# In the dense stages, the first down piece is split in the first unit instead of at the end of the stage before

## The reference, cut to what matters

```python
def swiglu(h, w_in, w_out):
    a, b = jnp.split(h @ w_in, 2, axis=-1)
    return (jax.nn.silu(a) * b) @ w_out

        h = adaln(x, norm_g[i, 0], shift[:, 0], scale[:, 0])
        x = x + MACARON_W * gate[:, 0, None] * swiglu(h, ffn_w_in[i, 0], ffn_w_out[i, 0])
```

## Time and profile before

| | us |
|---|---|
| median of 3 runs | 4208.21 (4208.19 to 4209.12) |
| profiled execution, its own time | 4201.7 |
| span of the profiled execution | 4199.9 |

### The profile page before, as it was taken

How to read it: one execution, slowest core, us unless ns; L and a number is a source line. 1 busy time by engine, 2 the same in 40 slices (tenths; PEclk the granted TensorE clock), 3 DMA queues, 4 the chain that set the end, 5 groups by cost and what they waited for, 6 DMA issues and landing times.

```text
span 4199.9 us, 69359 instructions
## 1 busy us (share of the span) xinstructions
PE 3884.0 (92%) x28940; PEld 3543.8 (84%) x28940; DVE 2685.7 (64%) x4863; ACT 1813.2 (43%) x3080; POOL 1456.4 (35%) x842
## 2 busy tenths in 40 slices
PE   7998998989989898979999989989999999999899
PEld 6658997679979867769999859989869998867699
DVE  4446776577777775567777867777657644665543
ACT  3233444334454442234545635444444444432343
POOL 2003443044434430034444423434314444320143
PEclk9759998699989999989999999999969999979899
DMA  5104662156646420027575415657516644210143
GB/s 207 56 16 177 259 263 103 59 192 261 254 167 264 179 95 13 1 106 271 226 271 197 151 51 200 267 211 271 190 53 241 264 168 158 96 41 1 45 168 115
DMA packets 63687, 664.37 MB, mean 158 GB/s; under 512 B 7056, under 2 KB 7568, under 8 KB 7952
## 3 DMA queue, kind: packets, MB, share of 16 engines
q1 hardware_dynamic: 63376, 659.94, 41.8%
HBM read 658.86 MB, written 1.05 MB: 157 GB/s over the span
## 4 chain that ended last, share of the span: by engine, by line
PE 79%; DVE 14%; ACT 4%; issue 1%; POOL 1%; DMA 0%; SPq 0%; DVEq 0%; ACTq 0%; POOLq 0%
PE pb L275 76%; PE pb L282 3%; DVE wp L228 2%; DVE wk L240 2%; DVE wk L228 2%; ACT wp L266 2%; DVE sq L240 1%; DVE ada_acc L240 1%; DVE hT L240 1%; ACT wk L266 1%; DVE sq L228 1%; DVE hx L240 0%; DVE hx L228 0%; POOL sq L228 0%; POOL wp L228 0%
## 5 line engine op out<-in xcount | busy, mean ns | idle before, releaser
L275 PE MATMUL pb<-hx,wp 128*128 128x256 f32 x15744 | 1995.8, 288 | 106.7 <-DVE hx L228 51.8
L275 PEld LDWEIGHTS pb<-hx,wp 128*128 128x128 f32 x15744 | 1956.4, 196 | 128.6 <-issue 106.6
L228 POOL TENSOR_TENSOR wp<-ring,wp 128x512 fp32r<-128x512 f32 (+1 forms) x596 | 1250.3, 2114 | 2005.8 <-ACT wp L266 2005.8
L266 ACT ACTIVATE wp<-ring 128x1024 fp32r<-128x1024 f32 x936 | 941.2, 1046 | 258.1 <-PE pb L275 250.9
L228 DVE TENSOR_TENSOR wp<-ring,wp 128x1024 fp32r<-128x1024 f32 (+1 forms) x670 | 796.8, 1206 | 359.3 <-ACT wp L266 355.3
L275 PE MATMUL pb<-ex,wp 128*128 128x256 f32 x5856 | 756.7, 287 | 19.4 <-DVE ex L228 19.4
L275 PEld LDWEIGHTS pb<-ex,wp 128*128 128x128 f32 x5856 | 728.9, 194 | 20.6 <-issue 18.0
L240 DVE SCALAR_TENSOR_TENSOR ada_acc<-ring,cact,ada_acc 128x384 f32<-128x384 f32 x576 | 529.8, 983 | 60.4 <-ACT ada_acc L266 60.2
L275 PE MATMUL pb<-wk 128*128 128x128 f32 (+8 forms) x3136 | 488.4, 327 | 16.8 <-ACT wk L266 7.7
L275 PEld LDWEIGHTS pb<-wk 128*128 128x128 f32 (+4 forms) x3136 | 339.8, 190 | 160.3 <-issue 96.6
L228 DVE TENSOR_TENSOR sq<-sq,pb 128x256 f32<-128x256 f32 (+1 forms) x360 | 161.4, 448 | 323.6 <-ACT sq L266 276.3
(11 more groups left out here) (179 smaller groups left out, 2821.2 us busy)
## 6 DMA issues: line engine op xcount, KB each, us to landing
ring<-weights SPq DMA_DIRECT2D x385, 1536.0 KB, 6.7
ring<-weights SPq DMA_DIRECT2D x41, 1024.0 KB, 4.8
ring<-weights SPq DMA_DIRECT2D x4, 512.0 KB, 10.2
cst<-consts SPq DMA_DIRECT2D x1, 2032.0 KB, 11.8
ring<-weights SPq DMA_DIRECT2D x1, 1280.0 KB, 5.5
prm<-params SPq DMA_DIRECT2D x1, 1258.0 KB, 7.4
ring<-weights SPq DMA_DIRECT2D x1, 1152.0 KB, 4.9
xT<-xT_in SPq DMA_DIRECT2D x1, 1024.0 KB, 4.8
```

What stands on the lines that cost most here:

```text
L228: return self.real.tensor_tensor(out, a, b, op) if self.real else Uncounted()
L266: return self.real.activation(out, a, func, bias=bias, scale=scale, accum_out=accum)
L275: return self.real.matmul(out, l, r, start=start, stop=stop, skip_group_check=skip)
```

## The change

`S.first` of a dense stage now holds only gate and up of unit 0. The down piece of unit 0 is put between the second and third piece of unit 1, on ACT and on POOL, by a helper that all three engines' loops now call. The slots, the ring's order, the matmuls and DVE's instructions stay as they are. The mixture-of-experts stages, which use the same functions with `first` = 2, get the same lists as before.

```diff
+    def next_unit(g, u):
+
+        n = g.pieces[u + 1]
+        return n[0:2] + [g.pieces[0][2]] + n[2:] if u == 0 == g.first else n
+
...
             elif u + 1 < g.units and u != g.first or g.first == 0 == u:
-                split_hi(e, g.pieces[u + 1])
+                split_hi(e, next_unit(g, u))
...
-                split_lo_v(e, g.pieces[u + 1])
+                split_lo_v(e, next_unit(g, u))
...
     def glu_pool(e, g):
         for u in range(1, g.units):
-            split_lo_g(e, g.pieces[u])
+            split_lo_g(e, next_unit(g, u - 1))
         split_lo_g(e, early(g.st + 1))
...
         G_ = plan_glu(st, 22, 0, unit, slot0, after)
-        S.first = G_.pieces[0]
+        S.first = G_.pieces[0][0:2]
```

## The result

| | median us (lowest to highest, executions) | profiled execution | its span |
|---|---|---|---|
| before | 4208.20 (4206.77 to 4209.12, 5) | 4201.7 | 4199.9 |
| after | 4227.25 (4221.20 to 4228.36, 5) | 4221.2 | 4219.4 |

The changed kernel is slower: ratio 1.0043, interval 1.0028 to 1.0057, 19.05 us between the medians and 19.5 between the spans. In a second set of executions (`change_again`) it was 1.0046 (1.0034 to 1.0058).

A forecast was written before the change was run, and what follows sets the result against it. PE, busy for 92% of the span, was taken to bound the kernel. 12.9 + 1.4 + 3.9 - 3.6 = 14.6 us over before gave 4222.8 us; the forecast's own range was 4216 to 4230, the wider one 4210 to 4231.

The forecast's parts named there:

- Part 1: Unit 0, six stages with an ada slice: POOL's second subtraction stretches DVE's second step, 2.15 us each, 12.9 us.
- Part 2: Unit 0, stages 15 and 17, no slice: POOL's second subtraction delays `ex`, PE loses 0.7 us each, 1.4 us.
- Part 3: Down of unit 0: longer PE pauses put all six slice stages at the slow clock, three more times 1.27, 3.9 us.
- The rivals' 4218.9: Unit 0's down: the clock does not follow the longer pause, three slow stages as now; 4218.9 us, chance 0.14.
- Part 4: Stage borders without the early split: gains of 1.6 (5 to 6), 1.25 (11 to 12), 0.77 (13 to 14); together 3.6 us.
- Part 5: Ring slot of unit 0's chunk is freed later, delaying unit 3's chunk; cover of 4.6 us, cost 0.
- DVE gets its steps in: Unit 0: DVE's steps get through between POOL's two subtractions; sum 0.8 us, 4209.0 us, chance 0.12.
- faster: Every border gains what stage 6's does (8 x 1.6 = 12.8 us), unit 0 hides the rest; 4195.4 us, chance 0.04.

The follow-up runs named there:

- twice_on_pool: Kernel before, with POOL doing the subtraction for unit 1's down piece twice in each dense stage, ACT and borders unchanged; 4233.94 us, ratio 1.0057.
- pool_waits_hid: Changed kernel, with POOL's second 128x1024 subtraction waiting until DVE has written the lo half of unit 0's hidden values, all eight stages; 4216.69 us, ratio 1.0023.
- pool_waits: Changed kernel, with POOL's second 128x1024 subtraction waiting until DVE has added up the ada slice, stages 15 and 17 as changed; 4229.01 us, ratio 1.0049.
- one_down: Changed kernel, with every unit's down piece split one unit later than before, so no unit has two; 4204.38 us, ratio 0.9994.
- warm_after: Changed kernel, with seven thrown-away float32 matmuls (128x256) on PE in unit 0's pause before the tiny matmuls; 4226.30 us, ratio 1.0039.
- warm_before: Kernel before, with three thrown-away float32 matmuls (128x256) on PE in unit 0's pause before the tiny matmuls; 4224.42 us, ratio 1.0043.
- dve_lo: Changed kernel, with DVE instead of POOL doing the whole subtraction for unit 0's down piece; 4229.26 us, ratio 1.0048.
- shift_2: Kernel before, with two float32 matmuls into an overwritten bank ahead of the last down of stage 9; 4210.01 us, ratio 1.0016.

## Why the prediction was right

It named 4222.8, and slower by over 0.2%; it is 4227.25, in the range, 4.4 us above. Step by step, in the profiles, where 14.6 were forecast and 19.5 came:

- **Part 1, unit 0.** Forecast 2.15 in each of six stages, 12.9. Measured 2.35 to 2.38, 14.2. The mechanism is as told: a second DVE step of 2.742 us behind POOL's second subtraction, two steps of six above 2 us, a pause of 3.62 in stage 8 and of 2.74 to 3.63 in the six (2.8 to 3.8 were named). `twice_on_pool` alone gives 2.12 to 2.27 of it, and `pool_waits_hid` takes all but 0.2 away. The 0.2 is what the step left out; it goes with the two more waits of PE's first down matmul. The rule of the Trainium skill ("SBUF — State Buffer", "Who interferes with whom"), that the earlier issued of the two holds the other for a whole instruction, agrees with the 2.742 and with the 1.90 of `ex` in `pool_waits`.
- **Part 2, stages 15 and 17.** Forecast 0.7 each; 0.75 and 0.76 came ahead of down of unit 0. In stage 17 it is the mechanism named, `ex` of 2.39 us and a wait of 0.60. In stage 15 only the size is right: `ex` is stretched too (2.40 us), but ends at 3395.20, and PE starts down at 3395.46, about when it would have come to it anyway: its products end one matmul's time (0.12 us) behind a last start at 3395.32, as they have run longer at the low clock. `one_down`, where `ex` was not late at all, loses 0.69 there. So two causes of about the same size lie over each other in stage 15: in `pool_waits`, whose stage 15 is the change's, the products were not longer and PE waited 0.59 us for `ex`. The step knew only one of them, and that they do not add is luck.
- **Part 3, the clock.** Forecast 3.9, measured 7.7: this is the term that was mis-sized. That all six stages would be slow was right. But each was counted as slow by 1.27, the form of before, and in stages 8, 11 and 14 the clock was low for 6.8 us instead of 3.4 and cost 2.5 to 2.7. Against before, down and the products behind it take 2.7 us more in stage 11 and 1.5 more in each of 9 and 12; 8 and 14, slow already and so put at nothing more, take 1.0 and 1.1 more. The bound of 9 held it. The rivals' 4218.9, with no more slow stages, fell. The Trainium skill's rule ("TensorE: Matmul & The Clock Gate", "What's actually happening") that idleness lowers the clock and activity brings it back agrees with `warm_after`, where the same delay without the idleness costs nothing of this term. It does not fit the loop of stage 10: in `warm_before` PE was busy for 61.76 of 64.86 us there and the clock stayed at the lower level.
- **Part 4, the borders.** Forecast -1.6, -1.25 and -0.77; measured -1.74 (stage 5), -1.25 (from DVE's last `ex` to PE's down in stage 11) and -0.78 (the norm's sum of stage 14). `one_down` has them without the loss.
- **Part 5, the ring.** Forecast 0, and 0 it was: the transfers issued from 1874 to 1890 landed in 6.9 us (median; 6.5 in the earlier trace rows), `one_down`, which frees unit 1's slot late as well, did not get slower, and ACT's one pause in the splits of unit 3 is on PE's use of a slot:

```profile
1888.16 2.01 ACT L266 ACTIVATE wp<-ring 128x1024 fp32r<-128x1024 f32 x2 [0.61 <-PE pb L275]
```

- **The rest.** The start (+1.6), which no edit touches, and gains that no part named in stages 7, 10 and 13 (-0.4, -0.5, and -0.95 beside the border) about cancel. So the 4.9 us between 14.6 and 19.5 are Part 3's 3.8 and Part 1's 1.3. The step from the profile to the median, forecast as 6.5 us, was 6.05. That these agree is chance: the profiled execution of `change_again` lies 1.9 us above its median, with 7.2 us more in the stretch ahead of all edits.

"DVE gets its steps in" (4209.0) and "faster" (4195.4) are ruled out by the tile row: the second step is 2.742 us, and DVE has no slack for it.

## What to carry to other kernels

Where two engines block each other on SBUF, ask of a moved instruction what it stands in front of and what it now directly follows: one POOL subtraction costs DVE one block, two in a row cost two, and a wait that puts it off only moves the block to the next DVE instruction unless it waits for the last one that PE needs. A stall of TensorE can cost twice, once as idle time and once in the matmuls at 1.2 GHz behind it; for 2.35 us more of the first, the second part grew by anything from nothing (stage 6) to 2.7 us (stage 11). Splitting work later than another piece that is waited for also adds waits to the consumer (with 0.2 us a stage here), so read the waits of the first instruction that needs it, not only the order.

## What the runs showed that was not expected

- The stretch at 1.2 GHz after a pause came in two lengths, 3.4 and 6.8 us. From the end of the products to down of unit 0 it was 4.3 us in stage 9, with the shorter (2094.78 - 2.96 to 2096.13), and 5.0 us in stage 8, with the longer (1864.41 + 13.25 to 1882.66); both forms came in the same stages in both profiles of the changed kernel. But the length of the pause does not decide it: 4.8 us gave the shorter in stage 11 of `twice_on_pool` and the longer in its stage 8, and 2.8 us the longer in stage 14 of `dve_lo`. Equal pauses also gave either none or the shorter: stage 11, with 2.6 us in both, is fast in the kernel before and slow in `shift_2` (+1.7), whose program is the same from stage 10 on. What decides between the forms stays open.
- A loop of small float32 matmuls (stage 10) can stay at 1.2 GHz for tens of us with PE busy for 95% of the time (61.76 of 64.86 us), and kernels that differ only hundreds of us ahead of it have that or not. In this kernel it is worth up to 25 us, more than anything that the change does. In experiments of a few us it must be read out of the profile first, as here by cutting at the norms.
